# Value products of a key piece one step earlier, and a group's closing sums with them, in the sample attention of a decoder layer

## What is computed

```python
s2 = jnp.einsum('bqgrd,bqgnd->bqgrn', q, ks, preferred_element_type=F32) * scale
s2 = s2 - slopes * dist_s
p2 = jax.nn.softmax(jnp.where(m2, s2, NEG), axis=-1)
o_slc = jnp.einsum('bqgrn,bqgnd->bqgrd', p2.astype(vs.dtype), vs)
...
o = g[..., 0:1] * o_cmp + g[..., 1:2] * o_slc + g[..., 2:3] * o_win
```

## Time and profile before

| | us |
|---|---|
| median of 3 runs | 3104.21 |
| lowest and highest run | 3104.07, 3106.21 |
| profiled execution, its own time | 3104.59 |
| span of its trace | 3102.5 |
| this stage in the trace | about 968 to 1085 |

### The profile page before, as it was taken

How to read it: one execution, slowest core, us unless ns; L and a number is a source line. 1 busy time by engine, 2 the same in 40 slices (tenths; PEclk the granted TensorE clock), 3 DMA queues, 4 the chain that set the end, 5 groups by cost and what they waited for, 6 DMA issues and landing times.

```text
span 3102.5 us, 56080 instructions
## 1 busy us (share of the span) xinstructions
PE 2926.2 (94%) x22989; PEld 2770.9 (89%) x22989; DVE 2329.7 (75%) x3588; ACT 1379.0 (44%) x2381; POOL 286.0 (9%) x290
## 2 busy tenths in 40 slices
PE   8999999989998888999988999999999999999995
PEld 7989999978776577879988999999999999999995
DVE  6656777866586626756578888888888888888887
ACT  5434555546455513433135444444444454444342
POOL 0010000024341201113320000000000000000010
PEclk9999999999999969999999999999999999999997
DMA  7654434368343942326334344444434455434333
GB/s 212 200 171 118 118 104 134 108 228 279 137 163 119 337 116 67 111 62 174 95 110 145 106 129 135 119 121 135 117 114 134 133 150 192 157 127 141 114 118 112
DMA packets 519317, 439.29 MB, mean 142 GB/s; under 512 B 35672, under 2 KB 476175, under 8 KB 512187
## 3 DMA queue, kind: packets, MB, share of 16 engines
q1 hardware_dynamic: 454742, 300.60, 33.7%
q0 software_dynamic: 20048, 82.12, 7.1%
q10 hardware_dynamic: 44272, 52.98, 5.1%
HBM read 377.43 MB, written 66.55 MB: 143 GB/s over the span
## 4 chain that ended last, share of the span: by engine, by line
PE 47%; DVE 6%; issue 1%; ACT 1%; DMA 0%; DVEq 0%; ACTq 0%
PE i L3075 40%; PE i L131 6%; DVE f_half L3552 1%; DVE x_blocks L3590 1%; PE i L3063 1%; DVE y_rows L3669 0%; DVE ln_parts L3596 0%; DVE y_rows L3674 0%; DVE h_rows L3585 0%; DVE resid L3445 0%; DVE resid L3444 0%; DVE x_blocks L3458 0%; PE i L3084 0%; DVE m_lo L3389 0%; DVE f_sum L3534 0%
## 5 line engine op out<-in xcount | busy, mean ns | idle before, releaser
L3075 PE MATMUL i<-x_blocks,f_half 128*128 128x272 f32 x10752 | 1359.3, 288 | 26.5 <-DVE h_rows L3585 12.7
L3075 PEld LDWEIGHTS i<-x_blocks,f_half 128*128 128x128 f32 x10752 | 1350.8, 189 | 30.8 <-DVE x_blocks L3590 14.3
L559 PE MATMUL a<-xb_in,w_half 128*128 128x272 f32 x4200 | 547.9, 292 | 9.2 <-DVE w_half L963 4.9
L559 PEld LDWEIGHTS a<-xb_in,w_half 128*128 128x128 f32 x4200 | 537.0, 190 | 18.4 <-issue 7.2
L3287 ACT CAST f_half<-w_ring 128x1024 fp32r<-128x1024 f32 (+2 forms) x370 | 346.4, 937 | 403.2 <-PE i L3075 340.7
L3552 DVE TENSOR_TENSOR f_half<-w_ring,f_half 128x1024 fp32r<-128x1024 f32 (+2 forms) x362 | 393.5, 1087 | 82.2 <-ACT f_half L3287 79.7
L3552 DVE TENSOR_TENSOR f_half<-f_sum,f_half 128x1024 fp32r<-128x1024 f32 (+2 forms) x148 | 159.5, 1078 | 80.9 <-ACT f_half L3287 80.8
L963 DVE TENSOR_TENSOR w_half<-w_ring,w_half 128x1024 fp32r<-128x1024 f32 x129 | 157.5, 1222 | 80.2 <-ACT w_half L697 79.9
L3287 ACT CAST f_half<-f_sum 128x1024 fp32r<-128x1024 f32 (+2 forms) x148 | 138.8, 938 | 156.4 <-PE i L3075 156.4
L697 ACT CAST w_half<-w_ring 128x1024 fp32r<-128x1024 f32 x125 | 131.4, 1051 | 108.8 <-PE a L559 104.9
L3047 POOL TENSOR_TENSOR f_half<-w_ring,f_half 128x512 fp32r<-128x512 f32 x8 | 11.9, 1492 | 1413.4 <-ACT f_half L3287 1413.4
(11 more groups left out here) (535 smaller groups left out, 4406.3 us busy)
## 6 DMA issues: line engine op xcount, KB each, us to landing
w_ring<-in_ffn_w_up_dram SPq DMA_DIRECT2D x88, 1024.0 KB, 6.5
w_ring<-in_w_in_dram SPq DMA_DIRECT2D x52, 1024.0 KB, 8.8
w_ring<-in_ffn_w_down_dram SPq DMA_DIRECT2D x24, 1536.0 KB, 6.9
w_ring<-in_w_o_dram SPq DMA_DIRECT2D x16, 1024.0 KB, 6.2
x_blocks<-s_blk ACTq DMA_DIRECT2D x17, 816.0 KB, 5.2
s_proj<-st ACTq DMA_DIRECT2D x48, 272.0 KB, 2.5
s_blk<-x_sums ACTq DMA_DIRECT2D x22, 544.0 KB, 6.3
kv_ring<-in_cmp_w_dram SPq DMA_DIRECT2D x16, 512.0 KB, 8.0
```

The costliest lines, as they stand in the source:

```text
L559: last = nc.tensor.matmul(ps[bank][:, 0:HT2], half(q, w)[:, k], XB[v[j]][:, k], start=j in (0, 1, 3) and k == 0 and i == 0, stop=k == HK - ...
L3075: last = nc.tensor.matmul(ps[bank][:, 0:HT2], half(e, j, wl_)[:, s], XB[:, x0 + s, xl_, BLK_OF[j]], start=start and s == 0 and i == 0, sto ...
```

## The change

TensorE's step i now ends with `values(i-1)` instead of `values(i-2)`, so that a piece's value products follow the transposes of its probabilities in the same step; the loop therefore starts them at step 1, and one call is left behind it instead of two. On DVE, `combine(G-1)` is called at c = 1 instead of c = 2, again ahead of that step's `take`. Nothing else is touched.

```diff
@@ TensorE
-                    if i >= 2:
-                        values(i - 2)
+                    if i:
+                        values(i - 1)
                     if c == 2 and G + 1 < NG:
                         misc_scores(G + 1)
...
                 turn_p(NC5 - 1)
-                values(NC5 - 2)
                 values(NC5 - 1)
                 out_turn(NG - 1)
@@ VectorE
                     if i == 0:
                         cmp_weights(0)
-                    if c == 2 and G:
+                    if c == 1 and G:
                         combine(G - 1)
                     if c == 3 and G + 1 < NG:
                         cmp_scores(G + 1)
```

## The result

| | before | after |
|---|---|---|
| median, us | 3106.21 (5 runs) | 3117.27 (5 runs) |
| lowest to highest | 3104.07 to 3108.7 | 3116.17 to 3123.07 |
| span of the trace | 3102.5 | 3115.2 |
| ratio to before, 95% interval | | 1.0038 (1.0026 to 1.0049) |

What follows compares the result with a forecast made beforehand. TensorE, busy in 94% of the span, was taken as the bound. Stall +5.1, end -0.1 and loads -1.2 gave +3.8 us, with 4 for the clock +7.8, so 3112.0 us; range 3105 to 3117.

Steps and rivals of the forecast that it cites:

- The stall: Groups 1 to 3, c = 1: TensorE waits 3.28 us for VectorE's key copy behind `combine`; net +5.1 us in all.
- The products' own copy: Value products waiting for the same step's copy of probabilities: covered by the key transposes, priced at 0.
- The start: First group, without `combine`: one more `values` in its steps fills a 1.0 us wait, 0.
- The end: Stage's end: one `values` follows the last exponential instead of two, but behind its copy, -0.1 us.
- The loads: Next stage's loads, released about 1059.9: VectorE's 1.21 us wait behind the last `combine` is covered, -1.2 us.
- The clock: Behind the three pauses TensorE falls to half clock for 3.4 us, two or three times: +3.0 to +4.5, taken as 4.
- the dearer rival: Half clock lasts, stretches of 6.8 us or further falls around the stage's end: 3115 to 3120 us; chance 0.06.
- The clock holds: Rival: full clock behind two or all three pauses, 3108.0 to 3109.5 us, within 0.2%; chance 0.22.
- the stall is short: Rival: `combine` cheaper at c = 1, stall of 1.4 to 2.5 us, 3103 to 3107 us; chance 0.07.
- faster: Rival: VectorE covers `combine` at c = 1, old stalls go, 3099.4 us or below 3098; chance 0.05.
- The rule on idle between bursts: Skill's rule: a loop idling TensorE between bursts returns to half clock every pass; all three pauses hit, sum 8.3 us.
- My last sign of being wrong: Prediction is wrong if later stages shift their own clock or waits by more than 2 us.

Runs made afterwards that it cites:

- x8: Changed kernel with 6 extra matmuls on TensorE between third and fourth key unit at c = 1; 1.0020 of the kernel before.
- x2: Changed kernel with 12 extra matmuls on TensorE between third and fourth key unit at c = 1; 1.0006 of the kernel before.
- x4: Changed kernel with the sums at c = 1 placed behind that step's key copy instead of ahead of its take; 1.0019 of the kernel before.
- x6: Kernel before with the sums at c = 2 cut in two, four adds from bank 7 moved behind the key copy; 1.0000 of the kernel before.
- x3: Changed kernel with the sums back at c = 2, value products still in the same step; 1.0038 of the kernel before.
- x1: Changed kernel with 24 extra matmuls on TensorE between third and fourth key unit at c = 1; 1.0028 of the kernel before.
- x9: Changed kernel with bank 6 copied out at c = 1 and the sums at c = 2 cut up around the key copy; 0.9985 of the kernel before.
- x10: The kernel before once more, unchanged, with its own profile; 0.9996 of the kernel before.

## Why the prediction was right and wrong

- **TensorE is the bound, the ring is not.** Right: no run has a wait of TensorE for a DMA in this stage.
- **The stall.** Forecast 3.28 us a group, pauses of about 3.15, 9.5 in all. Measured 3.26, 3.18 and 3.16, 9.6 in all. The wait at c = 2 is gone, as worked out. Three groups at full clock: +5.4 in x8, forecast +5.1.
- **The products' own copy.** Forecast 0 for the steady steps; there is no wait above 0.15 us there in the change's profile.
- **The start.** Forecast 0, measured +0.2. **The end:** forecast -0.1; from the last `scores` to L1967 (1966 after) it took 6.84 and then 6.71. **The loads:** forecast -1.2, and the 1.21 us are gone. SP's first load started at 1066.19 and not at 1059.9, because two groups at half clock lie ahead of it.
- **The clock, the step that failed.** "With 6 of 7, two or three of the three pauses are hit: +3.0 to +4.5. I take 4." All three were hit, and the cost was 7.5 us. The count was right, the length was not. I took 3.4 us at half clock for each fall; in both profiles of the change the first two lasted 6.8 us (6.3 and 6.8 of them behind the pause in the first profile) and the third 3.4. The rows had a hint: behind the pause at 2569 the mean was still 0.67 over a stretch where one of 3.4 us would have given 1 - 1.7 / 6.1 = 0.72. They stop too early; the trace of the kernel before goes on

```profile
2575.00:2576.50 1.50, 1.50 (x8) 1.50 (x8) 1.50 (x2) 0.38 (x1) 0.00 (x0) 0.50 0.20 73
2576.50:2578.00 1.50, 1.50 (x9) 1.50 (x8) 1.50 (x4) 1.48 (x3) 0.00 (x0) 0.55 0.00 0
```

and this fall lasts 6.8 us, as does the one behind the pause at 214. So two of the six falls that I counted were of the double length. An estimate from these six, at 1.5 and 3.1 us each, is 2.0 us a fall and 6 for three; that the case drew two long ones of three is beyond it. I had the double length in the bounds (9.3) and in the dearer rival, at 0.06, where two of three falls belong. With 7.5 the forecast would have been 3115.5 on the old median, and the range would have reached beyond 3120.
- **Rivals.** "The clock holds", "the stall is short" and "faster" did not happen. "Dearer" did in part: two of three falls had its length, and 3117.3 lies in its 3115 to 3120. x2 is the first of them made real, at 1.0006, inside what I called no change.
- **The rule on idle between bursts** (the Trainium skill, "TensorE: Matmul & The Clock Gate", "HAM oscillation — how this bites in real kernels") was quoted without the length of the idle time; the section's example has waits of about 3 to 5 us. For pauses of 3.2 us it gave all three falls, and that is what the traces show here. In x4, with pauses of 2.9 us, there was no fall in one of three places, and in the profile of x8, with 1.9, in none.
- **The rest.** Sum to the end of the stage: forecast 7.8, measured 11.6, of which the clock term explains 3.5. The median of before has itself moved from 3104.21 to 3106.21 with two more runs. It took both, the 3.5 us of the clock and these 2.0, to carry the time over the end of the range; with one of them alone it would lie inside. My last sign of being wrong, a later stage that shifts by more than 2 us, was met as well: the feed-forward part has 3.1 more in this one profile, a term that the sum did not have, and whether it belongs to the change stays open.

## What to carry to other kernels

A block of work on a helper engine costs what it pushes back behind it, so its place is chosen by how far that engine is ahead there: the same 3.54 us of sums cost 1.4 us at one step and 3.3 one step earlier, and next to nothing when cut in two around the urgent copy. A stall on TensorE must be priced with the clock it loses: here 3.2 us of pause took 2.5 us more on average behind it, and a pause of 1.3 took none. How long the clock stays down was the part that could not be read from the length of the pause. And before a stage is shortened, look at what its end waits for: x6 gained 4.3 us inside and met the loads.

## What the hardware showed that I had not expected

- Stretches at half clock came in two lengths behind pauses of one kind: 6.8 us twice and 3.4 once in each profile of the change, 3.4, 3.4 and none in x4. In x3, with pauses of 4.2, it was 6.9, 3.4 and 3.4. What decides which was not found.
- In six of the ten experiments' profiles (x1 to x4, x9, x10) a wait of 1.3 us for ScalarE's key copy stands at c = 3 (in x10's first group 0.6 us); in the other four and the two profiles of the case there is none, with the same program in x10 and before. It is in groups 0, 1 and 2 and not in group 3, and it stands behind `misc_scores`, which the last group does not run. The delay comes ahead of ScalarE: in group 1 of before, the key unit that starts at 1017.38 is copied from 1018.07, and in x10 the one that starts at 1015.24 only from 1017.35, and VectorE's `take` starts as late. The three groups of runs were on three chips, and all profiles of a chip agree. The cause stays open.
- A float32 matmul of 128 x 128 by 128 is two instructions of 0.115 us each in these traces, while a transpose of the same size is one.
